# Attention scores of two components or heads as one pair of matmuls, one exponential per pair, the triangle as a product

## The chip, the cores and the metric

The kernel runs on one Trainium2 chip, on all 8 cores. Each core computes one of the 8 batch entries by itself, and no data passes between cores. The metric is the device time in microseconds (us) of the slowest core.

## What is computed

A decoder trunk of four layers. Each layer is `x += 0.5*SwiGLU(norm(x))`, then `x += W_o [differential | forgetting | dilated](norm(x) W_in)`, then a second SwiGLU. The width is 1024 and the sequence 4096. The attention part, which is all that the change touches, is, cut down:

```python
# differential, 6 heads: two components q1,k1 / q2,k2 of width 32, one value v of width 64
p1 = softmax(where(causal, q1 @ k1.T * 32**-0.5, -inf)); p2 = the same with q2, k2
o  = rms_norm((p1 - lam * p2) @ v, g_sub, 1e-5) * (1 - lam_init)
# forgetting, 6 heads of width 64
p  = softmax(where(causal, q @ k.T * 64**-0.5 + (c[t] - c[s]), -inf));  o = p @ v
# dilated, 4 heads of width 64: windows (128,1), (512,4), (2048,16) merged by their denominators,
#   which is exp(scores) times a weight 0..3 that depends on t - s alone, normalised
```

## The kernel before

All work is issued by a Python program that writes out each engine's instructions in order. `Ctx.op` and `Ctx.group` put a wait in front of an instruction for each buffer (`Buf`) that it reads or writes and whose last user is not yet known to be done, and each engine executes its instructions in the order in which they were issued. The wait counts the own engine's instructions too: an instruction that writes a buffer last written by its own engine waits for that one's completion.

A layer has four phases: SwiGLU (`a`), projections (`p`), attention (`m`), SwiGLU (`c`). In the trace the tiles carry the layer and the phase: `L0m_pt` is tile `pt` of layer 0's attention.

`phase_attn` first loads constants and memsets (`va`: its columns 64 to 127 are ones, so that the value matmul also gives the denominator; `qz`: zero but for the rows of one component or head, so that a full 128-row matmul against `ks`, which holds four components or two heads, gives that component's scores alone). Then it makes a flat list of items. An item is one block of 128 keys (`kb`) against one block of 512 queries (`qb`, 0 to 7) for one unit. A unit is one component of a differential head, one forgetting head or one dilated head. Query block `qb` has `4*qb+4` key blocks (at most 20 in the dilated part); the last four are diagonal, and only 512, 384, 256 and 128 of their columns are computed. A layer has 1728 differential, 864 forgetting and 480 dilated items, in this order.

One loop over the items issues, for item `i`:

1. ScalarE: the exponential of item `i` from its score bank in PSUM into `pt` (L880; L876 in the forgetting part, with a bias).
2. In the dilated part, VectorE: `pt` times the weights `wt` (L886).
3. TensorE: the scores of item `i+2` (`emit_S`; L766, on the diagonal L761 and then L763, which adds a triangle of -30000 by a matmul of the identity with `tril`). Scores use four banks in turn. At the first item of a forgetting query block VectorE also makes the bias `bq` (L734).
4. TensorE: the value matmul of item `i-2` (`emit_PV`, L832), accumulated over the key blocks in one of three banks.
5. Work that was deferred until now.

At the last key block of the second component, `emit_PV` issues `diff_stage1`: on VectorE the reciprocal of the first component's denominator (L789), a product (L790), the same for the second (L792, L793), the difference (L795), and on GpSimd its square (L797). `diff_stage2` is deferred by `DEFER` = 22 items, though no more than one may be pending when the next one comes: TensorE sums the squares into a bank of its own, `psT` (L804), ScalarE takes the logarithm and an exponential (L806, L808), VectorE writes the result (L809). A forgetting query block ends with `plain_epilogue` at once (VectorE: L782, L784), a dilated one with the same after 6 items and with logarithm and exponential on ScalarE in place of the reciprocal (L777, L779).

The output projection (L926) follows.

Of the kernel before, what the change touches and what calls it, by code (L numbers as in the profile page):

```python
# [576 lines left out]
def phase_attn(c, g, sc, wo_d, lamq1_d, lamk1_d, lamq2_d, lamk2_d, gsub_d, lam_init, consts, x_src, x_dst, S, pfx,  # L577
# [4 lines left out]
    with ExitStack() as st:  # L582
# [67 lines left out]
        for i in range(2):  # L650
            c.op("pool", lambda e: e.memset(va[i][:, :, 64:128], 1.0), writes=[VA[i]])
        for i in range(4):
            c.op("pool" if i % 2 == 0 else "dve", lambda e: e.memset(qz[i][:], 0.0), writes=[QZ[i]])
        pm = g.psT[:].bitcast(F32)
        PM = g.PST
# [6 lines left out]
        for h in range(6):  # L662
            cd, hl = h // 2, h % 2
            ksl = cd % 2

            def loads(h=h, cd=cd, hl=hl, ksl=ksl):
                if hl == 0:
                    c.dma("sp", f"ld_ks{ksl}", ks[ksl][:], sc.kTd[cd * 128:(cd + 1) * 128, :], writes=[KS[ksl]])
                for pz in (2 * hl, 2 * hl + 1):
                    r = cd * 128 + pz * 32  # L670
                    c.dma("sp", f"ld_qz{pz}", qz[pz][pz * 32:(pz + 1) * 32, :], sc.qTd[r:r + 32, :], writes=[QZ[pz]])
                c.dma("sp", f"ld_va{h % 2}", va[h % 2][:, :, 0:64], vsrc[:, :, h * 64:(h + 1) * 64], writes=[VA[h % 2]])
# [392 lines left out]
```

How the kernel before makes its waits and increments, by code:

```python
    def wait(self, e, tok):  # L64
        if tok is None:
            return
        s, v = tok
        if v <= 0:
            return
        key = (e, s)
        if self.seen.get(key, 0) >= v:
            return
        self.eng[e].wait_ge(self.sems[s], v)
        self.seen[key] = v
        self.ninst += 1
# [29 lines left out]
    def op(self, e, fn, reads=(), writes=()):  # L105
        self._deps(e, reads, writes)
        ins = fn(self.eng[e])
        s = "c_" + e
        self.sem(s)
        self.cnt[s] += 1
        ins.then_inc(self.sems[s], 1)
        self.ninst += 1
        tok = (s, self.cnt[s])
        self._commit(tok, reads, writes)
        return tok
# [1 line left out]
    def group(self, e, fns, reads=(), writes=()):  # L117
        self._deps(e, reads, writes)
        ins = None
        for fn in fns:
            ins = fn(self.eng[e])
            self.ninst += 1
        s = "c_" + e
        self.sem(s)
        self.cnt[s] += 1
        ins.then_inc(self.sems[s], 1)
        tok = (s, self.cnt[s])
        self._commit(tok, reads, writes)
        return tok
# [1 line left out]
    def dma(self, e, semname, out, in_, reads=(), writes=(), **kw):  # L131
        self.sem(semname)
        self._deps(e, reads, writes)
        self.wait(e, (semname, self.cnt[semname]))
        ins = self.eng[e].dma_start(out=out, in_=in_, **kw)
        self.cnt[semname] += 16
        ins.then_inc(self.sems[semname], 16)
        self.ninst += 1
        tok = (semname, self.cnt[semname])
        self._commit(tok, reads, writes)
        return tok
```

The softmax here doesn't subtract the row's maximum and nothing guards it: scores larger than these inputs give would overflow.

## Time and profile before

| | us |
|---|---|
| median of 2 runs | 18979.94 (18912.4 to 19047.47) |
| span of the profiled execution, slowest core | 18680.2 |
| spans of the eight cores | 18600.2 to 18680.2 |
| TensorE busy | 16574.1 (89%) |
| ScalarE busy | 9004.0 (48%) |
| VectorE busy | 6278.7 (34%) |
| GpSimd busy | 929.4 (5%) |
| mean granted TensorE clock, slowest core | 0.956 |

The profile is of one execution. Busy time of TensorE counts matmuls from their issue to the end of their passage, and neighbours overlap, so it is more than the time that the engine needs. The shares are means over phases with different limits.

### The profile page before, as it was taken

How to read it: one execution, taken by the hardware profiler on the slowest of the kernel's cores; microseconds unless marked ns; L12 is line 12 of the kernel's file. 1: busy time of each engine (PE TensorE's matmuls, PEld its weight loads, DVE VectorE, ACT ScalarE, POOL GpSimd, SP SyncE). 2: the span in 40 equal slices, each digit the busy share in tenths (PEclk: the TensorE clock that was granted, in tenths of full speed). 3: DMA queues.
4: the chain of work that ended last, by engine and by line, in shares of the span. 5: the costliest groups of instructions: out<-in, count | busy, mean ns of one | idle time of the engine just before them, and what ended most of it. 6: DMA issues, size and time to landing. Idle time of an engine off the chain costs nothing.

```text
span 18680.2 us, 262548 instructions; the slowest of 8 cores (18600.2 to 18680.2 us)
## 1 busy us (share of the span) xinstructions
PE 16574.1 (89%) x75072; PEld 7111.5 (38%) x75072; DVE 6278.7 (34%) x7537; ACT 9004.0 (48%) x17109; POOL 929.4 (5%) x716
## 2 busy tenths in 40 slices
PE   8978999799997899979898889997989898998794
PEld 3433333244443333334444333333444343333341
DVE  2223444422222444532221344452222234445221
ACT  2214999422222599932221269992222227998121
POOL 0011000000001100000000110000000010000000
PEclk9989999999998999999999999999999999999997
DMA  4132001513114200151412310005141221001512
GB/s 87 52 84 64 10 13 23 116 59 84 55 50 95 53 12 12 23 124 54 88 55 61 88 40 12 16 20 132 55 90 55 67 85 29 10 17 34 126 55 92
DMA packets 854125, 1072.66 MB, mean 57 GB/s; under 512 B 339288, under 2 KB 529048, under 8 KB 844568
## 3 DMA queue, kind: packets, MB, share of 16 engines
q1 hardware_dynamic: 680240, 883.83, 15.8%
q0 software_dynamic: 172544, 172.03, 6.8%
q8 instruction: 710, 11.63, 0.3%
q14 instruction: 631, 5.17, 0.1%
HBM read 908.30 MB, written 319.36 MB: 66 GB/s over the span
## 4 chain that ended last, share of the span: by engine, by line
PE 80%; DMA 8%; ACT 4%; DVE 4%; issue 3%; another core or an unknown queue 1%; SPq 1%; POOL 0%; ACTq 0%; DVEq 0%; POOLq 0%
PE ps L832 16%; PE pp L295 13%; PE pp L299 13%; PE ps L327 12%; PE pp L766 12%; PE pp L520 4%; PE pp L528 3%; PE ps L562 2%; PE pp L761 2%; DMA out<-L3m_xr 1%; DMA fin_xt<-out 1%; DMA out<-L1m_xr 1%; PE pp L763 1%; DMA out<-L2m_xr 1%
## 5 line engine op out<-in xcount | busy, mean ns | idle before, releaser
L832 PE MATMUL ps<-L1m_pt,L1m_va 128*128 128x512 bf16 (+3 forms) x3072 | 1117.8, 364 | 35.4 <-DVE L1m_pt L886 16.4
L832 PE MATMUL ps<-L2m_pt,L2m_va 128*128 128x512 bf16 (+3 forms) x3072 | 1117.0, 364 | 32.2 <-DVE L2m_pt L886 15.5
L832 PE MATMUL ps<-L0m_pt,L0m_va 128*128 128x512 bf16 (+3 forms) x3072 | 1115.8, 363 | 32.6 <-DVE L0m_pt L886 16.4
L832 PE MATMUL ps<-L3m_pt,L3m_va 128*128 128x512 bf16 (+3 forms) x3072 | 1111.1, 362 | 32.7 <-DVE L3m_pt L886 16.4
L880 ACT ACTIVATE L1m_pt<-pp 128x512 bf16<-128x512 f32 (+3 forms) x2208 | 1043.0, 576 | 60.6 <-PE pp L763 22.5
L880 ACT ACTIVATE L2m_pt<-pp 128x512 bf16<-128x512 f32 (+3 forms) x2208 | 1043.0, 576 | 58.8 <-PE pp L763 21.6
L880 ACT ACTIVATE L0m_pt<-pp 128x512 bf16<-128x512 f32 (+3 forms) x2208 | 1043.4, 576 | 57.7 <-PE pp L763 20.3
L880 ACT ACTIVATE L3m_pt<-pp 128x512 bf16<-128x512 f32 (+3 forms) x2208 | 1042.8, 576 | 57.3 <-PE pp L763 20.1
L766 PE MATMUL pp<-L2m_qz,L2m_ks 128*128 128x512 bf16 (+3 forms) x1824 | 679.9, 373 | 55.6 <-ACT L2m_pt L880 55.5
L766 PE MATMUL pp<-L0m_qz,L0m_ks 128*128 128x512 bf16 (+3 forms) x1824 | 678.5, 373 | 56.2 <-ACT L0m_pt L880 55.8
L766 PE MATMUL pp<-L1m_qz,L1m_ks 128*128 128x512 bf16 (+3 forms) x1824 | 678.8, 373 | 55.7 <-ACT L1m_pt L880 55.5
L766 PE MATMUL pp<-L3m_qz,L3m_ks 128*128 128x512 bf16 (+3 forms) x1824 | 677.9, 372 | 55.7 <-ACT L3m_pt L880 55.5
L832 PEld LDWEIGHTS ps<-L1m_pt,L1m_va 128*128 128x128 bf16 x3072 | 295.3, 96 | 694.6 <-issue 643.3
L832 PEld LDWEIGHTS ps<-L2m_pt,L2m_va 128*128 128x128 bf16 x3072 | 295.1, 96 | 692.5 <-issue 640.0
L832 PEld LDWEIGHTS ps<-L0m_pt,L0m_va 128*128 128x128 bf16 x3072 | 295.2, 96 | 689.6 <-issue 638.2
L832 PEld LDWEIGHTS ps<-L3m_pt,L3m_va 128*128 128x128 bf16 x3072 | 294.7, 96 | 682.3 <-issue 628.8
L876 ACT ACTIVATE L0m_pt<-pp,L0m_bq 128x512 bf16<-128x512 f32 (+1 forms) x864 | 472.9, 905 | 40.3 <-DVE L0m_bq L734 34.3
L876 ACT ACTIVATE L1m_pt<-pp,L1m_bq 128x512 bf16<-128x512 f32 (+1 forms) x864 | 474.1, 884 | 36.5 <-DVE L1m_bq L734 25.7
L876 ACT ACTIVATE L2m_pt<-pp,L2m_bq 128x512 bf16<-128x512 f32 (+1 forms) x864 | 473.2, 904 | 36.2 <-DVE L2m_bq L734 29.3
L876 ACT ACTIVATE L3m_pt<-pp,L3m_bq 128x512 bf16<-128x512 f32 (+1 forms) x864 | 471.8, 909 | 32.7 <-DVE L3m_bq L734 27.8
L302 ACT ACTIVATE L0c_sg<-pp 128x512 f32<-128x512 f32 x176 | 105.1, 597 | 678.1 <-PE pp L295 669.8
L302 ACT ACTIVATE L1c_sg<-pp 128x512 f32<-128x512 f32 x176 | 105.1, 597 | 677.9 <-PE pp L295 677.6
(547 smaller groups left out, 29103.9 us busy)
## 6 DMA issues: line engine op xcount, KB each, us to landing
L0a_xt<-x SPq DMA_DIRECT2D x32, 512.0 KB, 4.0
L0a_xr<-x SPq DMA_DIRECT2D x64, 256.0 KB, 2.9
out<-L0a_xr SPq DMA_DIRECT2D x64, 256.0 KB, 2.3
L0p_xt<-out SPq DMA_DIRECT2D x32, 512.0 KB, 4.1
L0m_xr<-out SPq DMA_DIRECT2D x64, 256.0 KB, 3.9
out<-L0m_xr SPq DMA_DIRECT2D x64, 256.0 KB, 4.2
L0c_xt<-out SPq DMA_DIRECT2D x32, 512.0 KB, 3.9
L0c_xr<-out SPq DMA_DIRECT2D x64, 256.0 KB, 2.9
```

The costliest lines, as they stand in the source:

```text
L295: (lambda e, kc=kc: e.matmul(pg[:], wg[:, kc, fc * 128:(fc + 1) * 128], xnT[b][:, kc, :], start=(kc == 0), stop=(kc == 7)))
L299: (lambda e, kc=kc: e.matmul(pu[:], wu[:, kc, fc * 128:(fc + 1) * 128], xnT[b][:, kc, :], start=(kc == 0), stop=(kc == 7)))
L302: c.op("act", lambda e: e.activation(out=sg[fc % 2][:], in_=pg[:], func=AF.Silu), reads=[PG], writes=[SG[fc % 2]])
L327: (lambda e, fc=fc: e.matmul(py[:], hT[:, fc, tt * 128:(tt + 1) * 128], wd[:, fc, dh * 512:(dh + 1) * 512], start=(fc == 0), stop=(fc == N ...
L520: (lambda e, kc=kc: e.matmul(pa[:], wq[:, kc, col:col + 128], xnT[b][:, kc, :], start=(kc == 0), stop=(kc == 7)))
L528: (lambda e, kc=kc: e.matmul(pb_[:], wq[:, kc, rcol:rcol + 128], xnT[b][:, kc, :], start=(kc == 0), stop=(kc == 7)))
L562: (lambda e, kc=kc: e.matmul(pv[:], xnT[b][:, kc, tt * 128:(tt + 1) * 128], wv[:, kc, hf * 512:(hf + 1) * 512], start=(kc == 0), stop=(kc ...
L761: lambda e: e.matmul(sbk[:, col0:512], kt[0:K, kb * 128:(kb + 1) * 128], qt[0:K, q0 + col0:q0 + 512], start=True, stop=False),
L766: c.op("pe", lambda e: e.matmul(sbk[:, col0:512], kt[0:K, kb * 128:(kb + 1) * 128], qt[0:K, q0 + col0:q0 + 512], start=True, stop=True), r ...
L832: c.op("pe", lambda e: e.matmul(obk[:, col0:512], va[vs][:, kb, :], p[:, col0:512], start=it["first"], stop=it["last"]), reads=[P, VA[vs]] ...
L876: c.op("act", lambda e: e.activation(out=p[:, col0:512], in_=sbk[:, col0:512], func=AF.Exp, scale=hd["scale"], bias=bq[bi][:, kb:kb + 1]), ...
L880: c.op("act", lambda e: e.activation(out=p[:, col0:w1], in_=sbk[:, col0:w1], func=AF.Exp, scale=hd["scale"]), reads=SBKS, writes=[P])
```

## The change

- A differential item is now both components of a head, a dilated item both heads of a 128-row group: two score matmuls, each on the 32 or 64 rows of its component or head in `qs` and `ks`, side by side in one 1024-column tile of two banks. The zero-padded `qz` and its memsets go. There are 864 differential, 864 forgetting and 240 dilated items. Two such tiles take turns where four banks did.
- One exponential covers both halves (a pattern of two runs of `512-col0` columns). Value matmuls stay two for a pair, one per component or head, each into its own bank; the banks in turn are now four, `psT` among them, and the sum of squares goes into the first component's bank.
- The triangle is no longer added by a matmul: after the exponential of a diagonal item VectorE multiplies the 128 columns of the diagonal (both halves at once) by zeros and ones, `tri2`.
- `DEFER` is 11 items and `DIL_DEFER` 3. When a differential query block ends, all deferred work is issued first (`while deferred`), where one might stay pending.
- `va` has four buffers, two of them with their ones set by VectorE; `qs` holds 128 rows and is loaded whole.

The core of the diff (loads, allocation and the making of the constant are left out):

```diff
-DIL_DEFER = 6
+DIL_DEFER = 3
...
+        obank = [(g.ps[4], g.PS[4]), (g.ps[5], g.PS[5]), (g.ps[6], g.PS[6]), (g.psT[:].bitcast(F32), g.PST)]
...
+        def s_slot(n):
+            if n == 2:
+                state["sb"] += state["sb"] % 2
+                ti = (state["sb"] % 4) // 2
+                state["sb"] += 2
+                return g.pp[ti][:], [g.PS[2 * ti], g.PS[2 * ti + 1]]
+            si = state["sb"] % 4
+            state["sb"] += 1
+            return g.ps[si], [g.PS[si]]
...
-            if hd["mask"] == "causal" and j >= 0:
-                c.group("pe", [
-                    lambda e: e.matmul(sbk[:, col0:512], kt[0:K, kb * 128:(kb + 1) * 128],
-                                       qt[0:K, q0 + col0:q0 + 512], start=True, stop=False),
-                    lambda e: e.matmul(sbk[:, col0:col0 + 128], g.ident[:], tril[:], start=False, stop=True),
-                ], reads=[QTB, KTB, TRIL, g.IDENT], writes=[SBK])
...
+            c.group("pe", [
+                (lambda e, m=m, r0=r0, r1=r1: e.matmul(sbk[:, m * 512 + col0:(m + 1) * 512],
+                                                       ks[sl][r0:r1, kb * 128:(kb + 1) * 128],
+                                                       qs[sl][r0:r1, q0 + col0:q0 + 512], start=True, stop=True))
+                for m, (r0, r1) in enumerate(hd["rows"])], reads=[QS[sl], KS[sl]], writes=SBKS)
...
+            for m in range(nm):
+                vs = hd["vs"][m]
+                obk, OBK = cur[m]
+                c.op("pe", lambda e: e.matmul(obk[:, col0:512], va[vs][:, kb, :], p[:, m * 512 + col0:(m + 1) * 512],
                                               start=it["first"], stop=it["last"]), reads=[P, VA[vs]], writes=[OBK])
...
-                        while len(deferred) > 1:
-                            deferred.pop(0)[1]()
-                        diff_stage1(oa, OA, obk, OBK, par)
+                    while deferred:
+                        deferred.pop(0)[1]()
+                    diff_stage1(oa, OA, ob_, OB_, par)
+                    deferred.append((i + DEFER, (lambda h=hd["hh"][0], qb=qb, par=par, oa=oa, OA=OA:
+                                                 diff_stage2(h, qb, par, oa, OA))))
...
-        DEFER = 22
+        DEFER = 11
...
+                c.op("act", lambda e: e.activation(out=v3(p[:], col0, 512), in_=v3(sbk, col0, 512), func=AF.Exp,
                                                    scale=hd["scale"]), reads=SBKS, writes=[P])
...
+            if hd["kind"] == "dil":
+                off = q0 - kb * 128 + col0
+                for m in range(nm):
+                    c.op("dve", lambda e: e.tensor_tensor(out=p[:, m * 512 + col0:(m + 1) * 512],
+                                                          in0=p[:, m * 512 + col0:(m + 1) * 512],
+                                                          in1=wt[:, off:off + w], op=ALU.mult),
                          reads=[WT], writes=[P])
+            elif kb >= 4 * qb:
+                c.op("dve", lambda e: e.tensor_tensor(
+                    out=v3(p[:], col0, col0 + 128), in0=v3(p[:], col0, col0 + 128),
+                    in1=tri2[:].rearrange("p (m q) -> p m q", q=128)[:, 0:nm, :], op=ALU.mult),
+                    reads=[TRI2], writes=[P])
```

## Rows read from the trace of the kernel before

**Rows 1.** Stretches of layer 0's attention, all engines (x instructions; PEclk is the granted clock).

```profile
1705.00:2667.50 962.50, 897.59 (x3882) 362.18 (x3882) 457.09 (x286) 874.47 (x1821) 55.59 (x48) 0.99 0.06 12
2667.50:3181.20 513.70, 480.50 (x1924) 178.12 (x1922) 214.87 (x145) 473.18 (x866) 18.55 (x6) 0.95 0.12 21
3181.20:3468.50 287.30, 246.61 (x966) 92.23 (x964) 208.70 (x513) 265.14 (x547) 0.00 (x0) 0.99 0.08 17
```

**Rows 2.** The second differential head by query blocks: 0, 1, 2, and 3 to 7.

```profile
1869.13:1872.81 3.68, 3.64 (x21) 1.76 (x21) 3.36 (x1) 3.03 (x9) 0.00 (x0) 1.00 0.86 150
1872.81:1883.73 10.92, 8.48 (x43) 3.73 (x42) 10.20 (x8) 8.03 (x18) 1.03 (x1) 1.00 0.04 6
1883.73:1898.52 14.79, 12.73 (x60) 5.24 (x59) 11.14 (x10) 13.01 (x29) 2.70 (x2) 1.00 0.01 2
1898.52:2029.29 130.77, 124.51 (x531) 49.62 (x530) 51.78 (x32) 121.54 (x252) 5.16 (x5) 1.00 0.01 4
```

**Rows 3.** Timeline of the differential part, TensorE in the order of issue, with one norm (L804).

```profile
2204.57 0.38 PE L832 MATMUL ps<-L0m_pt,L0m_va 128*128 128x512 bf16 x1
...
2204.79 0.38 PE L766 MATMUL pp<-L0m_qz,L0m_ks 128*128 128x512 bf16 x1
...
2205.10 0.38 PE L832 MATMUL ps<-L0m_pt,L0m_va 128*128 128x512 bf16 x1
...
2205.93 0.40 PE L804 MATMUL psT<-L0m_tsq,ones64b 64*64 64x512 bf16 x1
...
2206.26 0.39 PE L761 MATMUL pp<-L0m_qz,L0m_ks 128*128 128x512 bf16 x1
```

**Rows 4.** ScalarE: 16 wide exponentials within 7.62 us (2591.69 to 2599.31); a 1024-column one elsewhere.

```profile
L880 ACT ACTIVATE L0m_pt<-pp 128x512 bf16<-128x512 f32 x16 | 7.8, 625 | 0.0
...
L167 ACT ACTIVATE L0a_junk<-L0a_xt 128x1024 bf16<-128x1024 f32 x32 | 33.6, 1050 | 6.2 <-DMA L0a_xt<-x 6.2
```

**Rows 5.** Groups in layer 0's attention (busy us, mean ns | idle before, releaser).

```profile
L763 PE MATMUL pp<-L0m_tril,ident 128*128 128x128 bf16 x576 | 129.4, 225 | 0.0
...
L792 DVE RECIPROCAL L0m_rec<-ps 64x512 f32<-64x512 f32 x48 | 161.2, 3359 | 218.6 <-PE ps L832 218.0
...
L886 DVE TENSOR_TENSOR L0m_pt<-L0m_pt,L0m_wt 128x256 bf16<-128x256 bf16 x32 | 9.3, 291 | 0.1
```

**Rows 6.** Timeline of one `diff_stage1`, VectorE and then GpSimd.

```profile
1874.54 3.36 DVE L789 RECIPROCAL L0m_rec<-ps 64x512 f32<-64x512 f32 x1
1878.00 0.68 DVE L790 TENSOR_TENSOR L0m_ta<-ps,L0m_rec 64x512 f32<-64x512 f32 x1
...
1883.04 0.74 DVE L795 SCALAR_TENSOR_TENSOR L0m_td<-L0m_tb,L0m_sm,L0m_ta 64x512 f32<-64x512 f32 x1 [0.17 <-DVE L0m_tb L793]
...
1884.04 1.29 POOL L797 TENSOR_TENSOR L0m_tsq<-L0m_td 64x512 bf16<-64x512 f32 x1 [8.24 <-PE ps L832]
```

**Rows 7.** Timeline of one `diff_stage2`: TensorE, then ScalarE up to its next exponential.

```profile
1880.71 0.40 PE L804 MATMUL psT<-L0m_tsq,ones64b 64*64 64x512 bf16 x1
...
1881.27 0.68 ACT L806 ACTIVATE L0m_tr<-psT,eps_sub 64x512 f32<-64x512 f32 x1 [1.20 <-PE psT L804]
...
1882.58 1.00 ACT L880 ACTIVATE L0m_pt<-pp 128x256 bf16<-128x256 f32 x3
```

**Rows 8.** Timeline of the forgetting part, second head, early query blocks.

```profile
2762.26 4.28 ACT L876 ACTIVATE L0m_pt<-pp,L0m_bq 128x512 bf16<-128x512 f32 x8 [3.82 <-DVE L0m_bq L734]
2763.09 0.58 PE L761 MATMUL pp<-L0m_qs,L0m_ks 65*128 65x512 bf16 x1 [3.60 <-ACT L0m_pt L876]
```

**Rows 9.** The stretch from there, all engines.

```profile
2761.20:2768.00 6.80, 4.91 (x17) 1.94 (x17) 6.55 (x5) 4.21 (x8) 2.49 (x1) 0.50 0.91 130
```

**Rows 10.** Dilated part, second head, all query blocks, all engines.

```profile
3256.07:3327.34 71.27, 61.16 (x241) 22.93 (x241) 51.41 (x129) 66.54 (x136) 0.00 (x0) 1.00 0.09 16
```

**Rows 11.** Timeline of VectorE in the dilated part, merged.

```profile
3421.88 2.38 DVE L886 TENSOR_TENSOR L0m_pt<-L0m_pt,L0m_wt 128x512 bf16<-128x512 bf16 x5
```

**Rows 12.** Timeline at the start of the attention phase.

```profile
1705.22 0.59 PE L761 MATMUL pp<-L0m_qz,L0m_ks 128*128 128x512 bf16 x1 [28.37 <-DMA L0m_qz<-s_qTd]
...
1710.91 0.58 PE L832 MATMUL ps<-L0m_pt,L0m_va 128*128 128x512 bf16 x1 [1.66 <-DMA L0m_va<-s_v]
```

More of the change, by code:

```diff
@@ L649, in phase_attn @@
                                               scalar2=None, op0=ALU.mult), reads=[], writes=[SM])
[L650 to L651 removed]
         for i in range(4):
[L653 to L655 removed]
+            c.op("pool" if i % 2 == 0 else "dve", lambda e: e.memset(va[i][:, :, 64:128], 1.0), writes=[VA[i]])
+        obank = [(g.ps[4], g.PS[4]), (g.ps[5], g.PS[5]), (g.ps[6], g.PS[6]), (g.psT[:].bitcast(F32), g.PST)]
         vsrc = sc.v.rearrange("(kb p) c -> p kb c", p=128)
@@ L663, in phase_attn, with loads @@
             cd, hl = h // 2, h % 2
-            ksl = cd % 2
-            def loads(h=h, cd=cd, hl=hl, ksl=ksl):
+            sl = cd % 2
+            vs = h % 4
+            def loads(h=h, cd=cd, hl=hl, sl=sl, vs=vs):
                 if hl == 0:
[L668 to L672, printed above, removed]
@@ L676, in phase_attn @@
+                c.dma("sp", f"ld_va{vs}", va[vs][:, :, 0:64], vsrc[:, :, h * 64:(h + 1) * 64], writes=[VA[vs]])
+            r = hl * 64
+            heads.append(dict(kind="diff", hh=[h, h], vs=[vs, vs], loads=loads, scale=SCALE_D, sl=sl,
+                              rows=[(r, r + 32), (r + 32, r + 64)]))
         for h in range(6):
-            sl = (6 + h) % 2
-            ksl = (3 + h) % 2
-            def loads(h=h, sl=sl, ksl=ksl):
+            sl = (3 + h) % 2
+            vs = (6 + h) % 4
@@ new lines, in loads @@
+                c.op("pool", lambda e: e.memset(ks[sl][64:65, :], 1.0), writes=[KS[sl]])
+                c.dma("sp", f"ld_va{vs}", va[vs][:, :, 0:64], vsrc[:, :, (6 + h) * 64:(7 + h) * 64], writes=[VA[vs]])
+            heads.append(dict(kind="fox", hh=[6 + h], fh=h, vs=[vs], loads=loads, scale=1.0, sl=sl, rows=[(0, 65)]))
+        for cc in range(2):
+            sl = (9 + cc) % 2
+            vs = [(2 * cc) % 4, (2 * cc + 1) % 4]
+            def loads(cc=cc, sl=sl, vs=vs):
+                c.dma("sp", f"ld_ks{sl}", ks[sl][:], sc.kTc[cc * 128:(cc + 1) * 128, :], writes=[KS[sl]])
+                c.dma("sp", f"ld_qs{sl}", qs[sl][:], sc.qTc[cc * 128:(cc + 1) * 128, :], writes=[QS[sl]])
+                for m in range(2):
+                    h = 12 + 2 * cc + m
+                    c.dma("sp", f"ld_va{vs[m]}", va[vs[m]][:, :, 0:64], vsrc[:, :, h * 64:(h + 1) * 64],
+                          writes=[VA[vs[m]]])
+            heads.append(dict(kind="dil", hh=[12 + 2 * cc, 13 + 2 * cc], vs=vs, loads=loads, scale=0.125, sl=sl,
+                              rows=[(0, 64), (64, 128)]))
```

148 lines of the change are left out of this document (38 added, 110 removed).

## The prediction, made before the change was timed

> **What bounds the kernel now.** I first cut the attention phase of layer 0 into its parts [rows 1]: 962.5, 513.7 and 287.3 us. That is 1763.5 us a layer, 38% of the span in four layers; nothing else is touched. In the differential part TensorE and ScalarE are both nearly always busy, so I looked at which of them makes the beat. Value matmuls follow each other by 0.53 us though a score matmul leaves after 0.22 [rows 3]: each waits for its predecessor on the same bank to complete, and its weight load starts only then. ScalarE alone could do better: 16 exponentials in 7.62 us are 0.476 each [rows 4]. So an off-diagonal item costs 0.53 us, two of them 1.05, set by TensorE's own wait. The table by query blocks then shows a second regime [rows 2]: block 1 takes 10.92 us with VectorE busy for 10.20 of them. Small blocks are bound by `diff_stage1`: 9.24 us from the start of L789 (1874.54) to the end of L795 (1883.78) [rows 6]. The other blocks hide most of it, because the first reciprocal starts when the first component is done, one unit before the second; VectorE then idles 218.6/48 = 4.6 us before the second reciprocal [rows 5].
>
> **Exponentials and scores.** The pair's exponential: from below 0.476 + (1.050 - 0.625) = 0.90 us, from above the 1.05 that a 1024-column one takes alone [rows 4]; I take 0.90, since the beat, not the latency, counts. On the diagonal the pairs are 1024, 768, 512 and 256 columns wide: 0.90 + 0.69 + 0.48 + 0.26 = 2.33. No row of before has two matmuls in disjoint row groups. TensorE needs per pair 0.22 (side by side) to 0.43 (one after the other) for scores and 0.43 for values: 0.65 to 0.86. Both are below 0.90, so ScalarE would make the beat, and a pair gains 0.15 over 1.05. The 576 triangle matmuls a layer, 225 ns each [rows 5], leave an engine that no longer sets the beat: nothing. Their replacement on VectorE, 0.29 for 256 columns [rows 5], has two items of cover (`PV` follows two items later), as long as VectorE is free.
>
> **The norm comes too early.** This is the large term. Now both components end together, so all of `diff_stage1` comes after the last value matmul: 9.24 us, then 0.26 to GpSimd's start and 1.29 for the squares [rows 6]: 10.8 after the first reciprocal starts. `diff_stage2` is issued 11 items after the last one, but the last value matmul is itself issued two items late, so only nine exponentials, 9 x 0.90 = 8.1 us, lie between. In ScalarE's queue the logarithm stands ahead of the next exponential; in TensorE's queue the sum of squares stands ahead of the next scores. Both wait. Let r be the start of the first reciprocal: the item that was just starting then is 1.65 us old (1.05 for its exponential, 0.1 of handing over, 0.31 from scores to values [rows 3], 0.2 for the last narrow value matmul). The sum of squares starts at r + 10.95, and the next exponential 1.87 later [rows 7], at r + 12.8. Of the next block's N items, and the first one after it, N - 14 full pairs and the diagonal are left, about 0.5 is lost (an estimate: 0.31 + 0.43 on TensorE, less the 0.26 of the narrowest exponential) where narrow pairs leave only two score tiles to refill, and 1.65 closes the circle. A block takes 12.8 + (N-14) x 0.90 + 2.33 + 0.5 + 1.65: for blocks 3 to 7 (N = 16 to 32) 19.1, 22.7, 26.3, 29.9, 33.5, together 131.5 against 130.77 [rows 2]. The whole gain of the wide exponential is given back.
>
> **Small blocks.** Block 0 of heads 2 to 6 starts while VectorE is in the previous head's `diff_stage1`. The triangle products of its items 2 and 3 are queued behind it, the value matmul of item 2 waits for them, and behind that everything on TensorE. Then `while deferred` issues the previous norm ahead of the new `diff_stage1`: its last step, 0.74, stands ahead of the new reciprocal in VectorE's queue. From r to r: (a) 10.95 + 1.87 + 0.1 + 0.74 = 13.7; (b) block 1: the triangle products of items 8 to 11 wait 9.55, item 8's values follow, one more pair of scores and its exponential (to 11.5) before item 11's values (12.2), then the norm 0.15 + 1.87, then 0.85: 15.1; (c) block 2: the norm at 10.95, three exponentials to 15.05, scores and values: 15.6. Sum 44.4 against 3.68 + 10.92 + 14.79 = 29.4 [rows 2]: 15 more, in five heads. The first head has no predecessor: about 7.5 more.
>
> Differential part: 6 x 0.7 + 5 x 15 + 7.5 = +87 us a layer.
>
> **The clock.** Where TensorE was idle for 3.60 us in the forgetting part [rows 8], the granted clock was 0.50, that is 1.2 GHz, over the next 6.8 us [rows 9]; in the differential part it was 1.00 from block to block [rows 2]. The new stalls are of 8, 6 and 3 us in each head, and in each of 30 larger blocks two of 2.2 and 2.5 us around the sum of squares. At half clock a pair needs 0.43 + 0.86 = 1.3 in place of 0.90, so 6.8 us lose up to 2. I take 2 a head for the small blocks (most hides behind VectorE) and 1 for each of 30 others (bounds 0 and 2): 12 + 30 = +42.
>
> **Forgetting part.** ScalarE sets its beat, and stays. The triangle products go behind `plain_epilogue` in the first two blocks. There the bias already waits for VectorE, 3.82 us before the exponential [rows 8]; three or four more products of 0.22 to 0.29 delay it by 0.9. Five times that and 3 us behind the last `diff_stage1`: +7 (0 to 20).
>
> **Dilated part.** VectorE has two weight products per pair. Five in a row take 2.38: 0.49 each with the wait between [rows 11]. The second product writes the tile that the first wrote, so it waits for its completion (0.1, as between L789 and L790 [rows 6]): 0.43 + 0.1 + 0.43 + 0.06 = 1.02 for a pair, over ScalarE's 0.90 and just below 2 x 0.53 of before. With diagonals (3.3) and epilogues, two on ScalarE and VectorE, a block of 20 is 16 x 1.02 + 3.3 + 1.5 + 1 = 22.1, and all eight 136, against 2 x 71.27 = 142.5 [rows 10]. Twice: -13 (-47 if ScalarE set the beat).
>
> **Start, queues.** SyncE issued the loads of `qz` behind memsets; the first scores waited for them, the first values for `va` [rows 12]. Now `qs`, four times the bytes of one `qz` piece, needs no memset, and `va` goes out earlier behind it; only the second head's `va` waits for VectorE's memset, with nothing behind it. 0, plus or minus 3. Later loads run one head ahead.
>
> **Sum.** 87 + 42 + 7 - 13 = +123 us a layer, +492 in four. Against the profiled span of 18680 this is 19172; the median of the runs, 18980, lies 300 above that span, and I keep that distance: 19470.
>
> **Rivals.**
> (1) *ScalarE never waits*: the squares are ready when the norm is reached. Then a head is 119.7 of exponentials + 4 of tails + 8 x 1.31 = 134 against 160.2, and the dilated part goes to its bound: -156 - 47 = -203 a layer, 18170. For it: ScalarE's busy share; before, the norm's wait on ScalarE was only 1.20 [rows 7]. Against it: 10.8 is more than the 8.5 at which it decides (from the end of the last values to the norm's place on TensorE).
> (2) *Gains and losses near balance*: the clock holds and the dilated part reaches ScalarE's bound: 87 + 7 - 47 = +47 a layer, 19170. For it: no drop of the clock in [rows 2]. Against it: the stalls become longer.
> (3) *The pair doesn't run side by side and TensorE makes the beat*, so the change doesn't do what its scores promise. Switching shape may cost: from the 64-row L804 to the next 128-row matmul are 0.33, not 0.22 [rows 3]. Two such steps a pair: 4 x 0.215 + 2 x 0.115 = 1.09, 0.19 more on 50 pairs a head after the norms: with the clock lower, about +70 a layer, 19750. The Trainium skill, TensorEngine Tiling (Array Packing), section Tiling Modes, says that changing the tiling mode drains TensorE, here twice a pair; the 0.33 agrees with that.
>
> **Chances.** Forecast 0.50, (1) 0.12, (2) 0.25, (3) 0.13. The range leaves out (1) and the tails: 18900 to 19900; the forecast's own, from the clock's bounds, 19300 to 19700. Two per cent, about what a measurement of this kernel can tell from no change, are 380 us: slower begins at 19360. From (3) and most of the forecast: slower 0.53; same 0.35 from (2) and the forecast's lower end; faster 0.12 from (1).
>
> **What would show it.** Right: L806 waits on ScalarE for the sum of squares by 2 us or more in each block, 48 times a layer, released in the end by GpSimd's squares; L832 waits for the new products on VectorE in blocks 0 to 2, 44 us a head; a granted clock below 1.00 in the differential part; weight products at 1.02 a pair; off-diagonal exponentials 0.90 apart. The forecast is wrong if ScalarE's exponentials run on through the norms (1), if a differential head takes 165 us or less, or if pairs come 1.1 us apart with TensorE never idle (3).

## The result, and the profile after

The changed kernel takes 20484.69 us (median of 2 runs, 20373.54 to 20595.84), 1.077 times the kernel before (95% interval 1.059 to 1.096). It is slower, as forecast, but by 1505 us where the forecast had 490, and outside the range. The span of its profiled execution is 20372.0 us on the slowest core, against 18680.2.

In parts of the experiments' executions all cores of a die show a granted clock of 0.81; stretches in which that is seen are left out of the readings below, so times are given by stage and layer rather than for whole runs.

The stretches of layer 0's attention after, differential, forgetting and dilated part, answer to [rows 1]. The columns are the stretch and its length, then the busy time of TensorE, its weight loads, VectorE, ScalarE and GpSimd (x instructions), the granted TensorE clock, the DMA share and GB/s:

```profile
1696.16:3053.03 1356.87, 1151.51 (x3496) 209.58 (x3495) 506.66 (x475) 858.26 (x958) 52.38 (x48) 0.57 0.03 7
3053.03:3594.38 541.35, 495.45 (x1731) 165.47 (x1729) 246.66 (x336) 477.86 (x865) 18.56 (x6) 0.92 0.13 21
3594.38:3872.91 278.53, 228.27 (x955) 58.50 (x956) 206.64 (x510) 244.93 (x301) 0.00 (x0) 0.86 0.06 15
```

The differential part has grown by 394 us and the forgetting part by 28. The dilated part has lost 6: the 287.3 of [rows 1] run 3 us past its last exponential, at which the stretch above ends, and cut there they are 284.2. That is +416 a layer, 1664 in four, against 1692 between the two spans. The loss is in one stage, and the column that has changed most there is the clock: 0.57 where [rows 1] have 0.99. The second differential head by query blocks (0, 1, 2, and 3 to 7) answers to [rows 2]:

```profile
1912.56:1926.88 14.32, 5.41 (x19) 1.17 (x18) 10.21 (x9) 4.95 (x6) 1.03 (x1) 0.50 0.00 0
1926.88:1943.76 16.88, 10.80 (x35) 2.10 (x34) 11.22 (x11) 7.99 (x11) 1.03 (x1) 0.50 0.00 0
1943.76:1962.46 18.70, 16.79 (x51) 2.96 (x50) 10.37 (x11) 11.93 (x15) 1.03 (x1) 0.50 0.00 1
1962.46:2143.04 180.58, 164.47 (x487) 28.79 (x486) 54.10 (x53) 119.00 (x131) 5.16 (x5) 0.55 0.01 3
```

Blocks 0 to 2 are what was forecast in kind (49.9 for 44.4). Blocks 3 to 7 are not: 180.6 for a forecast of 131.5 and some clock. Two stretches within them, same columns, show the two states that TensorE is in, and that the lower one lasts:

```profile
2015.40:2029.10 13.70, 10.52 (x50) 2.89 (x49) 8.83 (x5) 9.59 (x11) 1.03 (x1) 1.00 0.01 2
2029.10:2138.30 109.20, 101.54 (x279) 16.44 (x278) 22.53 (x22) 72.65 (x77) 2.06 (x2) 0.50 0.00 1
```

The timeline around that change (start, length, engine, line, operation, names, shape, idle time before and what ended it) shows what TensorE did around the fall at 2029.10: it stood 2.63 us for the squares before it, and another 2.55 us, for the first exponential behind the norm, after it.

```profile
2027.67 1.03 POOL L765 TENSOR_TENSOR L0m_tsq<-L0m_td 64x512 bf16<-64x512 f32 x1 [29.78 <-DVE L0m_td L763]
2028.96 0.47 PE L772 MATMUL ps<-L0m_tsq,ones64b 64*64 64x512 bf16 x1 [2.63 <-POOL L0m_tsq L765]
2029.53 0.68 ACT L774 ACTIVATE L0m_tr<-ps,eps_sub 64x512 f32<-64x512 f32 x1 [4.27 <-PE ps L772]
...
2031.98 0.61 PE L733 MATMUL pp<-L0m_qs,L0m_ks 32*128 32x512 bf16 x2 [2.55 <-ACT L0m_pt L842]
```

And 70 us later, still at 0.50, one pair after the other:

```profile
2100.63 0.61 PE L733 MATMUL pp<-L0m_qs,L0m_ks 32*128 32x512 bf16 x2
...
2101.17 0.61 PE L793 MATMUL ps<-L0m_pt,L0m_va 128*128 128x512 bf16 x1
...
2101.39 1.02 ACT L842 ACTIVATE L0m_pt<-pp 128x1024 bf16<-128x1024 f32 x1 [0.48 <-PE pp L733]
2101.57 0.63 PE L793 MATMUL psT<-L0m_pt,L0m_va 128*128 128x512 bf16 x1
2102.13 0.61 PE L733 MATMUL pp<-L0m_qs,L0m_ks 32*128 32x512 bf16 x2
```

A pair takes 1.50 us, 2100.63 to 2102.13. TensorE now makes the beat (0.54 from scores to values, 0.40 to the second values, 0.56 to the next scores) and ScalarE waits 0.48 in each. At 1.00, in the same head, the same three steps take 0.32, 0.23 and 0.31, together 0.86:

```profile
2139.80 0.39 PE L733 MATMUL pp<-L0m_qs,L0m_ks 32*128 32x512 bf16 x2
...
2140.12 0.39 PE L793 MATMUL ps<-L0m_pt,L0m_va 128*128 128x512 bf16 x1
...
2140.35 0.38 PE L793 MATMUL psT<-L0m_pt,L0m_va 128*128 128x512 bf16 x1
...
2140.66 0.34 PE L733 MATMUL pp<-L0m_qs,L0m_ks 32*128 32x384 bf16 x2
```

There ScalarE sets the beat: five wide exponentials in a row take 4.69 us (2015.98 to 2020.67) where one takes 1.02, so they are 0.92 apart.

### The profile page after: what moved, and what is told of

It reads as the page before. It is cut to its first block, busy times and chain, and to the rows that moved or that the text cites. A ratio compares the mean times of both kernels' runs of the same rounds, so it can differ in the third digit from the quotient of the medians.

```text
span 20372.0 us, 242532 instructions; the slowest of 8 cores (20116.4 to 20372.0 us)
## 1 busy us (share of the span) xinstructions
PE 17586.9 (86%) x72768; PEld 6337.3 (31%) x72768; DVE 6612.9 (32%) x9073; ACT 8880.1 (44%) x12693; POOL 888.4 (4%) x708
## 4 chain that ended last, share of the span: by engine, by line
PE 77%; DMA 7%; DVE 6%; ACT 5%; issue 3%; another core or an unknown queue 1%; SPq 1%; POOL 0%; ACTq 0%; DVEq 0%; POOLq 0%
PE ps L793 13%; PE pp L733 13%; PE pp L295 12%; PE pp L299 12%; PE ps L327 11%; PE psT L793 5%; PE pp L520 4%; PE pp L528 3%; PE ps L562 2%; DMA fin_xt<-out 1%; DMA out<-L3m_xr 1%; DMA out<-L2m_xr 1%; DMA out<-L1m_xr 1%; DMA out<-L0m_xr 1%
## 5 line engine op out<-in xcount | busy, mean ns | idle before, releaser
L842 ACT ACTIVATE L0m_pt<-pp 128x1024 bf16<-128x1024 f32 (+1 forms) x1104 | 1010.6, 954 | 345.5 <-PE pp L733 338.5
L842 ACT ACTIVATE L2m_pt<-pp 128x1024 bf16<-128x1024 f32 (+1 forms) x1104 | 1008.5, 954 | 337.1 <-PE pp L733 328.1
L842 ACT ACTIVATE L1m_pt<-pp 128x1024 bf16<-128x1024 f32 (+1 forms) x1104 | 1008.9, 955 | 336.2 <-PE pp L733 329.3
L842 ACT ACTIVATE L3m_pt<-pp 128x1024 bf16<-128x1024 f32 (+1 forms) x1104 | 1004.9, 957 | 315.6 <-PE pp L733 309.6
L733 PE MATMUL pp<-L1m_qs,L1m_ks 32*128 32x512 bf16 (+8 forms) x3072 | 895.0, 468 | 206.4 <-ACT L1m_pt L842 169.6
L733 PE MATMUL pp<-L0m_qs,L0m_ks 32*128 32x512 bf16 (+8 forms) x3072 | 889.7, 467 | 210.8 <-ACT L0m_pt L842 169.2
L733 PE MATMUL pp<-L2m_qs,L2m_ks 32*128 32x512 bf16 (+8 forms) x3072 | 884.2, 464 | 209.8 <-ACT L2m_pt L842 169.5
L733 PE MATMUL pp<-L3m_qs,L3m_ks 32*128 32x512 bf16 (+8 forms) x3072 | 873.5, 457 | 211.4 <-ACT L3m_pt L842 170.6
L793 PE MATMUL ps<-L0m_pt,L0m_va 128*128 128x512 bf16 (+3 forms) x2176 | 947.6, 479 | 97.9 <-DVE L0m_pt L852 64.8
L793 PE MATMUL ps<-L1m_pt,L1m_va 128*128 128x512 bf16 (+3 forms) x2176 | 943.6, 477 | 96.9 <-DVE L1m_pt L852 63.2
L793 PE MATMUL ps<-L2m_pt,L2m_va 128*128 128x512 bf16 (+3 forms) x2176 | 937.5, 474 | 100.3 <-DVE L2m_pt L852 67.1
L793 PE MATMUL ps<-L3m_pt,L3m_va 128*128 128x512 bf16 (+3 forms) x2176 | 924.2, 468 | 97.5 <-DVE L3m_pt L852 64.2
L733 PEld LDWEIGHTS pp<-L0m_qs,L0m_ks 32*128 32x128 bf16 (+2 forms) x3072 | 204.4, 97 | 1117.7 <-issue 1108.5
L733 PEld LDWEIGHTS pp<-L2m_qs,L2m_ks 32*128 32x128 bf16 (+2 forms) x3072 | 204.8, 97 | 1103.3 <-issue 1093.7
L733 PEld LDWEIGHTS pp<-L3m_qs,L3m_ks 32*128 32x128 bf16 (+2 forms) x3072 | 205.4, 97 | 1090.8 <-issue 1081.9
L733 PEld LDWEIGHTS pp<-L1m_qs,L1m_ks 32*128 32x128 bf16 (+2 forms) x3072 | 204.4, 97 | 1084.9 <-issue 1072.2
L793 PE MATMUL psT<-L1m_pt,L1m_va 128*128 128x512 bf16 (+3 forms) x896 | 431.6, 482 | 1.1
L793 PE MATMUL psT<-L2m_pt,L2m_va 128*128 128x512 bf16 (+3 forms) x896 | 426.2, 476 | 1.5 <-DVE L2m_pt L852 0.3
```

The source lines that it names most:

```text
L733: (lambda e, m=m, r0=r0, r1=r1: e.matmul(sbk[:, m * 512 + col0:(m + 1) * 512], ks[sl][r0:r1, kb * 128:(kb + 1) * 128], qs[sl][r0:r1, q0 + ...
L793: c.op("pe", lambda e: e.matmul(obk[:, col0:512], va[vs][:, kb, :], p[:, m * 512 + col0:(m + 1) * 512], start=it["first"], stop=it["last"] ...
L842: c.op("act", lambda e: e.activation(out=v3(p[:], col0, 512), in_=v3(sbk, col0, 512), func=AF.Exp, scale=hd["scale"]), reads=SBKS, writes=[P])
```

## Experiments

The numbers of all kernels, each from one layer's attention, all cut at the same exponentials. "us at 0.50" is the time within the differential part at which the granted clock was 0.50.

| kernel | differential us | clock | us at 0.50 | forgetting | dilated |
|---|---|---|---|---|---|
| before | 962.5 | 0.99 | 11 | 513.1 | 284.2 |
| after | 1356.9 | 0.57 | 1169 | 541.4 | 278.5 |
| e1: before, own rows | 1803.8 | 0.50 | 1804 | 512.8 | 478.4 |
| e10: before, changes of shape | 1143.0 | 0.99 | 12 | 513.3 | 316.6 |
| e2: after, 128 rows | 1143.6 | 0.87 | 298 | 541.5 | 279.1 |
| e6: after, filler | 1268.7 | 0.82 | 456 | 544.5 | 311.2 |
| e4: after, norm later | 1321.3 | 0.57 | 1123 | 543.1 | 278.4 |
| e15: after, norm in three | 1181.4 | 0.64 | 860 | 543.1 | 278.4 |
| e7: e2, norm later | 1032.9 | 0.92 | 167 | 539.1 | 278.1 |
| e8: e2, triangle by matmul | 1127.4 | 0.88 | 273 | 513.4 | 271.4 |
| e5: padded pairs, norm later | 1037.6 | 0.91 | 184 | 511.1 | 285.7 |
| e11: e5, norm after 18 | 1034.0 | 0.91 | 178 | 509.3 | 285.1 |
| e12: blocks 0 to 2 single | 1004.0 | 0.94 | 124 | 512.2 | 286.4 |
| e16: e12, norm in three | 903.8 | 0.98 | 42 | 507.8 | 284.5 |
| e14: e16 with own rows | 1042.1 | 0.77 | 482 | 511.0 | 284.6 |

### Are row groups enough to lower the clock?

The first kernel is the one before with one edit: a score matmul reads its own 32 or 64 rows of the same operands; the rest held zeros.

```diff
-            K = hd["K"]
+            r0, r1 = hd["rows"][it["ui"]]
-                                                      kt[0:K, kbm * 128:(kbm + 1) * 128],
-                                                      qt[0:K, q0:q0 + 512], start=True, stop=True))
+                                                      kt[r0:r1, kbm * 128:(kbm + 1) * 128],
+                                                      qt[r0:r1, q0:q0 + 512], start=True, stop=True))
```

> The kernel before, with one part of the change alone: a score matmul reads only the 32 rows (differential) or 64 rows (dilated) of its component or head, one item at a time; the triangle matmul, the norm, the banks and all waits stay as before. Theory A (the new waits at the norm and the triangle products let the clock fall, the row groups cost only the change of shape): no new wait, so the granted clock stays above 0.94; a change of shape twice an item costs at most 0.1 us more on 2208 items a layer, 19000 to 19850 us in all. Theory B (score matmuls on few rows and their changes of shape keep the clock low, waits only start it): the clock is below 0.90 although there is no new wait, differential items take about 1.1 us where they are at half clock, and the time is above 20500 us.

Layer 0's stretches, columns as above:

```profile
1723.97:3527.78 1803.81, 1799.04 (x3884) 361.98 (x3884) 456.97 (x286) 1004.17 (x1823) 53.65 (x48) 0.50 0.03 6
3527.78:4040.61 512.83, 483.48 (x1920) 178.01 (x1918) 212.92 (x145) 473.63 (x866) 18.55 (x6) 0.94 0.11 21
4040.61:4519.02 478.41, 474.95 (x960) 99.14 (x959) 212.95 (x512) 300.41 (x544) 0.00 (x0) 0.50 0.04 10
```

Two groups of TensorE in its differential part (busy us, mean ns | idle before, releaser):

```profile
L833 PE MATMUL ps<-L0m_pt,L0m_va 128*128 128x512 bf16 (+2 forms) x1725 | 995.1, 577 | 2.6 <-DMA L0m_va<-s_v 2.6
L767 PE MATMUL pp<-L0m_qz,L0m_ks 32*128 32x512 bf16 x1344 | 808.7, 602 | 1.1 <-ACT L0m_pt L881 0.5
```

TensorE is busy for 1799 of 1804 us, and yet the granted clock is 0.50 throughout; the untouched forgetting part is as before. So the clock can be held at 1.2 GHz with hardly a wait. What let it fall is another matter: it fell at 1696, while TensorE stood for the loads ahead of the part, and in the dilated part at 4044.5, 4 us after its start and 0.4 us into a wait of 3.46 us. The same shape in small amounts does not keep it down: the next kernel is the one before with a 32-row, 16-column matmul, overwritten at once, ahead of each wide score matmul.

```diff
+            tiny = [] if hd["kind"] == "fox" else [
+                lambda e: e.matmul(sbk[:, col0:col0 + 16], kt[0:32, kb * 128:(kb + 1) * 128],
+                                   qt[0:32, q0 + col0:q0 + col0 + 16], start=True, stop=True)]
-                c.group("pe", [
+                c.group("pe", tiny + [
```

> The kernel before, with a 32-row matmul of 16 columns added ahead of each score matmul of the differential and dilated parts, overwritten by it: two changes of shape an item, as with row groups, but the wide matmuls all fill 128 rows. If the little-filled array of the wide score matmuls lets the clock fall, the clock stays above 0.95 in the differential part here, and an item takes 0.1 to 0.25 us more: 1130 to 1400 us a layer. If the changes of shape do, the clock is near 0.5 there, as with the row groups alone, and the part takes 1700 us or more.

The differential part of layer 0:

```profile
1745.17:2888.16 1142.99, 1101.13 (x5612) 465.47 (x5612) 456.40 (x286) 979.60 (x1822) 55.59 (x48) 0.99 0.05 10
```

The timeline of TensorE in it:

```profile
2300.35 0.38 PE L836 MATMUL ps<-L0m_pt,L0m_va 128*128 128x512 bf16 x1
2300.66 0.18 PE L760 MATMUL pp<-L0m_qz,L0m_ks 32*128 32x16 bf16 x1
2300.77 0.39 PE L770 MATMUL pp<-L0m_qz,L0m_ks 128*128 128x512 bf16 x1
2301.00 0.38 PE L836 MATMUL ps<-L0m_pt,L0m_va 128*128 128x512 bf16 x1
```

The clock stays at 0.99, and the part takes 180 us longer over 1728 items, 0.105 each: in the rows 0.42 lie between values and scores where [rows 3] have 0.22, and 0.23 between scores and values where they have 0.31. The Trainium skill, TensorEngine Tiling (Array Packing), section Tiling Modes, says that a change of tiling mode drains TensorE; the 0.105 for two changes agrees with a cost of that kind, though it also holds the small matmul itself. So changes of shape with so small a matmul cost time and leave the clock alone; what holds the clock down in e1 is wide matmuls on few rows.

### The same in the changed kernel

Pairs on all 128 rows (each score is then the sum over all that the 128 rows hold, so the numbers differ and the work on ScalarE and VectorE does not), and the changed kernel with one more, overwritten, 128-row matmul ahead of each pair:

```diff
-                for m, (r0, r1) in enumerate(hd["rows"])], reads=[QS[sl], KS[sl]], writes=SBKS)
+                for m, (r0, r1) in enumerate(hd["rows"] if nm == 1 else [(0, 128)] * 2)], reads=[QS[sl], KS[sl]], writes=SBKS)
...
+            fill = [] if nm == 1 else [
+                lambda e: e.matmul(sbk[:, col0:512], ks[sl][:, kb * 128:(kb + 1) * 128],
+                                   qs[sl][:, q0 + col0:q0 + 512], start=True, stop=True)]
```

> The changed kernel, with one part undone: both score matmuls of a pair read all 128 rows (so they come one after the other, and each gives the sum over all components of the row block: what the softmax sees is changed, the work and its order are not). All waits of the change stay. Theory A: those waits still let the clock fall, mean clock 0.86 or less, 20000 us or more. Theory B: the clock recovers soon after each wait, mean clock above 0.92; a pair takes 0.92 us, a differential head about 175 us in place of 230, and the time is 19200 to 19600 us, near the forecast of +123 us a layer.

> The changed kernel with one matmul added ahead of each pair of scores: 128 rows, as wide as the scores, into the first of their two banks, overwritten by the pair. TensorE has more to do (0.86 us a pair at full clock, under ScalarE's 0.92), and no wait is taken away. Theory A: the waits let the clock fall as now, and at half clock a pair takes 1.9 us in place of 1.5: 21500 us or more. Theory B, in the form that the array is too little filled: the clock comes back after each wait, mean above 0.90, time below 19900 us. Theory B, in the form that the changes of shape by themselves keep it low: as theory A.

The first takes 213 us off the differential part (table) and leaves 181 over the kernel before. The second adds 864 matmuls to the part and still takes 88 off, at a clock of 0.82. Both land between their theories (the first at a clock of 0.87 and 191 us a head, where theory B had over 0.92 and 175). Both keep every wait that the program issues. So more than half of the loss hangs on the rows that the score matmuls use.

### What lets it fall, what keeps it down

The changed kernel with `DEFER` 14 and the norm issued behind `diff_stage1` in place of ahead of it:

```diff
-                    while deferred:
-                        deferred.pop(0)[1]()
                     diff_stage1(oa, OA, ob_, OB_, par)
+                    while deferred:
+                        deferred.pop(0)[1]()
-        DEFER = 11
+        DEFER = 14
```

> The changed kernel with the norm deferred by 14 items in place of 11, and with the new block's reciprocals issued ahead of an older norm where a block ends early. This takes away the wait for the squares in blocks 3 to 7 and part of that in blocks 0 to 2. Theory A: without these stalls the clock stays up, mean above 0.90, time 19600 us or less. Theory B: the clock falls all the same, mean 0.83 to 0.87, time 20000 to 20450 us (some 2 us for each of 48 norms a layer).

The part took 1291 to 1321 us, where the changed kernel's layers have 1323 to 1366, with the clock as low. The long wait of this version is looked at below; with it gone as well (the norm in three, 17 items later), the changed kernel is:

```diff
+                    for late, fn in ((0, diff_norm_a), (2, diff_norm_b), (3, diff_norm_c)):
+                        deferred.append((due + late, lambda fn=fn, args=args: fn(*args)))
```

> The changed kernel (all pairs on their own 32 or 64 rows, triangle on VectorE) with one thing changed: the norm is behind the next block's epilogue, 17 items after its block, its sum of squares two items ahead of the logarithm and its exponential one behind it. Theory 'waits let the clock fall, row groups keep it down': with the long waits of the larger blocks gone the clock falls in the small blocks only, and comes back late; differential part 1120-1240 us a layer with a granted clock of 0.68-0.80 (changed kernel: 1340 at 0.58). Theory 'row groups alone': 1280 or more at 0.62 or less. Theory 'waits alone': under 1080 at 0.85 or more.

Measured 1125 to 1247, at clocks of 0.58 to 0.69 where that theory had 0.68 to 0.80. Blocks 6 and 7 of the first head, and then the same blocks of the second:

```profile
1843.20:1869.29 26.09, 24.80 (x116) 6.64 (x114) 10.75 (x11) 25.51 (x31) 1.03 (x1) 1.00 0.00 1
1869.29:1898.37 29.08, 28.22 (x131) 7.74 (x130) 11.01 (x13) 28.41 (x35) 1.03 (x1) 1.00 0.00 1
2030.60:2071.43 40.83, 40.83 (x116) 6.66 (x114) 10.74 (x11) 28.32 (x31) 1.03 (x1) 0.50 0.00 1
2071.43:2116.40 44.97, 44.77 (x131) 7.69 (x130) 11.12 (x13) 31.30 (x35) 1.03 (x1) 0.53 0.07 24
```

The same instructions run in one of two states. At 1.00 ScalarE makes the beat; at 0.50 TensorE does, never idles, and the clock does not come back. Here a wait lets the clock fall, and the row groups keep it down: in the second head it fell behind a wait of 2.01 us (1964.48 to 1966.49) and stayed at 0.50 for the next 147 us. The last of this set has the row groups in blocks 3 to 7 only, in a version almost without long waits there (e16 below):

> As the version with the norm cut in three, with one edit: in the pairs of blocks 3 to 7 each score matmul reads the 32 rows of its component alone, as in the changed kernel (same operands otherwise, the rows left out are zeros). Theory 'wide matmuls on few rows hold the clock': without any long wait of TensorE the granted clock of the differential part still falls to 0.50-0.65 in blocks 3 to 7, pairs come 1.5 us apart in place of 0.92, and the part takes 1150-1250 us a layer. Rival 'it was the waits': with the waits gone the clock stays above 0.90 and the part within 30 us of the version it is made from.

Both theories missed: 938 to 1048 us, 34 to 144 over the version it is made from (904), 217 to 499 us of them at 0.50. In one layer block 4 took 29.63 us in the first head and 18.66 in the second (19.27 on 128 rows, so at 1.00 own rows are a little faster). How much is lost depends on when the clock falls, which differs from head to head.

The trace also shows that no long wait is needed for the fall. Around the end of block 5 of the second head e14 and e16 have the same short waits, none over 0.43 us on own rows and 0.41 on 128. The 7 us there and the 34 behind them, first on own rows (layer 0, core 3 of e14), then on 128 (layer 0, core 0 of e16):

```profile
1966.20:1973.20 7.00, 5.82 (x34) 1.91 (x34) 1.55 (x2) 6.04 (x9) 0.00 (x0) 1.00 0.00 1
1973.20:2007.30 34.10, 34.10 (x100) 6.15 (x99) 8.17 (x6) 23.31 (x25) 1.03 (x1) 0.50 0.00 0
```

```profile
1931.40:1938.40 7.00, 5.79 (x34) 2.76 (x34) 1.52 (x2) 6.09 (x9) 0.00 (x0) 1.00 0.00 1
1938.40:1972.50 34.10, 32.95 (x150) 11.99 (x149) 16.12 (x10) 33.39 (x38) 1.03 (x1) 1.00 0.00 1
```

TensorE was busy for as long before (5.82 and 5.79 us), and only on own rows the clock falls, in four of the six heads of this layer. So the row groups do both: they keep the clock down, and they let it fall where 128 rows do not.

### The rest: norm, triangle, small blocks

On 128 rows less hangs on the clock (298 us at 0.50 in e2), so the other parts are read there. Norm as in e4, and, in a second kernel, the triangle by matmul again as in the kernel before:

> The changed kernel with 128-row score matmuls (each gives the sum over all components of the row block, so what the softmax sees is changed) and with the norm after 14 items, behind the new block's reciprocals. Against the one with 128 rows alone (differential part 1143 us a layer at a clock of 0.87 on undisturbed cores): the forecast's step for the norm, 2.35 us for each of 30 blocks and the step behind the old norm in the small ones, says 1040 to 1080. If the norm's wait is hidden behind something else: 1110 or more.

> The changed kernel with 128-row score matmuls (again with sums over components) and the triangle added by matmuls as before; the norm stays early. Against 1143 us a layer in the differential part and 541 in the forgetting part with 128 rows alone: if the triangle products cost what the forecast's chain of small blocks says, 1080 to 1110, and the forgetting part gives back most of its 33 us, to about 510 to 515 (the forecast gave it only 7). If the stalls in small blocks are the reciprocals alone: 1130 and 535 or more.

The norm's place is worth 111 us a layer (1033, just under the 1040 to 1080 expected of it). The triangle as a product costs little in the differential part, 1127 to 1133 us in the layers of e8 against 1142 to 1147 in e2; with the forecast's chain e8 should have come to 1080 to 1110. It costs all of the 28 in the forgetting part: ScalarE's waits there, 40.3 us in the kernel before, are in the changed kernel

```profile
L838 ACT ACTIVATE L0m_pt<-pp,L0m_bq 128x512 bf16<-128x512 f32 (+1 forms) x862 | 476.6, 725 | 61.8 <-DVE L0m_bq L723 30.9 <-DVE L0m_pt L852 21.9 <-PE pp L733 5.4
```

Both together, with `qz` padded as before so that the result is the reference's again, and the dilated heads one by one:

> What is left of the change when each suspected loss is taken out: differential items as pairs with one wide exponential, but both score matmuls on all 128 rows against zero-padded queries; the triangle by matmul as before; the norm after 14 items, behind the new block's reciprocals; dilated heads one at a time as before. If the row groups, the triangle products and the early norm are the whole loss, the differential part of an undisturbed core falls to 880 to 960 us a layer (962 before, 1340 after) at a clock above 0.95, the forgetting part to 505 to 515 (541 after), and the kernel takes 0.98 to 1.00 of the time before. If the pair itself is at fault (both components end together, and two score tiles take turns in place of four banks), the differential part stays above 1000 us and the kernel is slower than before by 1% or more.

A miss: 1038, 75 over the kernel before with every forecast cause removed. The next two were to settle why:

```diff
-        DEFER = 14
+        DEFER = 18
...
+                if hd["kind"] == "diff" and qb < SINGLE:
+                    comps = [[0], [1]]
```

> As the zero-padded version (all differential components in pairs on 128 rows, triangle by matmul, norm behind the next block's epilogue), with the norm 18 items after the block's end in place of 14. In the trace of the 14-item version the step from the first reciprocal to the logarithm of the norm is 12.2 us, and 14 items leave only 12 exponentials of 0.92 before it, 11.0 us: TensorE still stood for 3.0 us in every larger block, and the granted clock fell to 0.50 behind it. Theory 'norm still too early': with 18 items (16 exponentials, 14.7 us) the wait and the drops go from blocks 4 to 7; blocks 3 to 7 of a head come from 132 us to 115 or less, the differential part from 1036 to 925-960 us a layer with a granted clock above 0.94. Rival 'pairs are no faster than components one by one': the differential part stays at 1020-1040. Small blocks 0 to 2 stay at 41 us a head in both.

> As the version with the norm after 18 items, but query blocks 0 to 2 keep the two components one after the other (as in the kernel before, norm after 22 items into a bank of its own), and only blocks 3 to 7 take them as a pair. Theory 'two separate prices, the exposed epilogue in small blocks and the norm's place in large ones': blocks 0 to 2 come back to 30 us a head (from 41) and blocks 3 to 7 stand at 113-118 (before: 131), so the differential part takes 860-900 us a layer against 962 before, and the whole 250-400 us less than the kernel before. Rival 'pairs are no faster': blocks 3 to 7 at 130 or more, differential part 955 or more, no gain.

Four items more changed nothing (1034), and the theory behind these two was wrong about the large blocks (132 us a head in both). Blocks 0 to 2 came to 37 us a head in the second, from 41, where 30 was expected; what holds the rest is not shown. The timeline of the first shows what holds the large blocks; the squares have been ready for 4 us, and yet:

```profile
2176.65 0.59 PE L806 MATMUL ps<-L0m_pt,L0m_va 128*128 128x512 bf16 x2
...
2177.17 0.40 PE L785 MATMUL ps<-L0m_tsq,ones64b 64*64 64x512 bf16 x1
2177.72 0.68 ACT L787 ACTIVATE L0m_tr<-ps,eps_sub 64x512 f32<-64x512 f32 x1 [1.65 <-PE ps L785]
2178.50 0.63 ACT L789 ACTIVATE L0m_tr<-L0m_tr 64x512 f32<-64x512 f32 x1
2179.03 1.91 ACT L855 ACTIVATE L0m_pt<-pp 128x1024 bf16<-128x1024 f32 x2
...
2180.18 0.83 PE L741 MATMUL pp<-L0m_qz,L0m_ks 128*128 128x512 bf16 x2 [2.61 <-ACT L0m_pt L855]
```

The norm is a round trip. With two score tiles the scores of item i+2 wait for exponential i; the sum of squares is issued behind them and the values of i-2, the logarithm behind the sum, and exponential i+1 behind the logarithm. ScalarE stands 1.65 us, then TensorE 2.61, and in the next 3.4 us the clock is 0.54. The kernel before had four score banks as cover: there the logarithm mostly waited 0.5 to 1.2 us, 1.20 in [rows 7]. So the norm was cut in three: the sum two items ahead of the logarithm, its exponential one behind it.

```diff
+                    for late, fn in ((0, diff_norm_a), (2, diff_norm_b), (3, diff_norm_c)):
+                        deferred.append((due + late, (lambda fn=fn, args=args: fn(*args)), npair[0] - 1))
```

> As the hybrid (differential blocks 0 to 2 one component after the other, blocks 3 to 7 as pairs on 128 rows), with the norm cut in three: the sum of squares is issued on TensorE two items ahead of the logarithm on ScalarE, and the exponential of the norm one item behind the logarithm. In the hybrid and in the 18-item version ScalarE stood 1.65 us ahead of the logarithm and TensorE 3.0 us behind it, although the squares had been ready for 4 us: with two score tiles the sum of squares is behind the scores of item i+2, which wait for exponential i, and exponential i+1 is behind the logarithm. Theory 'two score tiles make the norm a round trip': the 1.65 us and the drop of the clock behind the 3.0 us go; blocks 3 to 7 come from 131.6 us to 113-119 a head, the differential part from 1008 to 900-935 a layer at a granted clock above 0.96, and the whole to 100-250 us under the kernel before. Rival 'the pair is no faster in steady state': blocks 3 to 7 stay at 128 or more, the differential part at 985 or more.

This came in as the first theory had it: 901 to 907 us a layer. The same kernel once more:

> The same kernel as the hybrid with the norm in three. Differential part 902-907 us a layer as before, 55-60 under the kernel before; forgetting and dilated parts unchanged at 511 and 285. Four layers: 220-250 us less than the kernel before, a ratio of 0.987-0.989, if both run without the third clock level. Rival: the gain is given back elsewhere in the layer (ratio 0.995 or more).

Layer 0's differential part, and in it blocks 3 to 7 of the second head:

```profile
1695.16:2598.96 903.80, 829.75 (x3881) 320.42 (x3880) 455.47 (x284) 829.61 (x1102) 54.04 (x48) 0.98 0.06 12
...
1879.40:1994.75 115.35, 110.73 (x527) 41.95 (x525) 46.74 (x31) 112.20 (x131) 5.16 (x5) 1.00 0.02 5
```

The first four cores, span and mean granted clock:

```profile
core 0: 18404.5 us, clock 0.954
core 1: 18429.8 us, clock 0.953
core 2: 18376.3 us, clock 0.955
core 3: 18409.7 us, clock 0.953
```

Blocks 3 to 7 of a head take 115.35 us where [rows 2] have 130.77, and the spans of these four cores are 18376 to 18430 against 18600 to 18680 before: 1.3% less by the middles of the two. So a pair with one wide exponential does pay, on full rows, in large blocks, and with the norm out of its way.

## Why the prediction was wrong, step by step

**The clock: the step that failed.** The prediction had drops of 6.8 us behind each stall, as in [rows 9], and +42 a layer. It weighed the row groups for their speed alone (side by side or not, shape changes) and took over from [rows 9] that the clock comes back by itself. With row groups it does not: 1169 us of layer 0's differential part were at 0.50, and taking the row groups out gives back 213 (e2). It also falls more easily: in e14 behind waits of 0.43 us at most, where the same waits on 128 rows leave it at 1.00 (e16). Even with the bound of 2 us per block (72 a layer) the term was a third of that. The half-clock pair was also low, 1.3 against 1.50, since the steps between shapes stretch as well.

**The norm too early: right, and too small.** L774 waits on ScalarE, and the sum of squares for GpSimd's squares, as forecast. On 128 rows, blocks 3 to 7 take 144 us (e2) against 131.5, with some clock in it. Its own 111 us a layer (e7) are only its lateness; the round trip, 100 more (e12 to e16), was not in the sum. The row for it was there: [rows 7] show 1.87 from the sum to the next exponential, but the prediction did not ask what four score banks had hidden and two would not.

**Small blocks: right in size.** Forecast 44.4 a head; 49.9 in the changed kernel, 47.7 on 128 rows with the norm as early (e2, mean of five heads). The chain through the triangle products was not needed for it: without them these blocks still take 43.2 (e8).

**Wide exponential, scores side by side: right.** 0.90 to 0.92 a pair at full clock for 0.90; the two score matmuls of a pair start 3 to 6 ns apart.

**Triangle: too dear in the differential part** (e8, above), **too small in the forgetting part** (+28 for +7, over the bound of 20). The products wait in VectorE's queue, and ScalarE behind them, in more blocks than the first two.

**Dilated part: near, by luck.** 139.6 and 138.9 us for two heads, forecast 136; -6 a layer for -13. The weight products do not set 1.02 a pair: ten of them in a row take 4.62 us (3659.69 to 3664.31), 0.92 a pair, so at full clock ScalarE and VectorE keep the same beat. Part of what that would have gained went to a clock of 0.86, which the forecast did not have there. **Start: right.** From the last projection matmul to the first exponential of layer 0 are 30.7 us, before 28.6 (means of eight cores); forecast 0, plus or minus 3.

**The median** lies 113 us above the span, where 300 was taken over from before.

**Rivals.** (3) had the right symptom, TensorE making the beat, for a wrong reason: pairs do run side by side, and at full clock TensorE's pair is 0.86, not 1.09. Its shape changes are real (e10), but hidden behind ScalarE until the clock falls. (1) fell with the norm, and (2) with the clock.

## What to carry to other kernels

Before score matmuls are cut to the rows that they need, look at what the granted clock does with them in a stretch with no waits: columns saved on TensorE are worth nothing if it then runs at 1.2 GHz. When fewer, wider tiles replace several small ones, follow every side job (here the norm) through each engine's queue again, since the tiles in flight were its cover. And an epilogue that was half hidden because two results ended one after the other comes out whole when they end together. Of this the experiments show only a part: going back to one after the other in the small blocks gave back some 4 of the 12 us a head (e12).
